# Attention probabilities of 6 of 16 pairs of heads turned by VectorE in 32x32 blocks and carried by DMA, in place of TensorE transposes

## The chip, the cores and the metric

One core of one Trainium2 chip runs the whole program, in one launch. The metric is the device time of an execution in microseconds (us). The kernel before took 1525.12 us in the median of three runs.

## The reference

Two sequences of 512 tokens with 1024 columns (`x_prompt` and `x_sample`) go through the same single layer with the same weights, all in float32:

```python
u = rmsnorm(h, norm_mix_g)
h = h + neighbourhood_attention(u, w_qkv, rpb, w_o)
u = rmsnorm(h, norm_ffn_g)
h = h + expert_choice_ffn(u, router_w, w_gate, w_up, w_down)
return rmsnorm(h, final_norm_g)
```

The attention has 16 heads of 64 columns. The tokens stand on a grid of 8 rows by 64 columns, and each token attends to the 8 rows of the 16 grid columns around it, with a bias per head and offset: `p = softmax(q k^T * 64**-0.5 + bias)`, then `p v`, then a product with `w_o`. The feed-forward part has 16 experts, each of which takes the 64 tokens of each sequence that score highest for it, through `silu(x w_gate) * (x w_up)` and `w_down` (1024 by 2048 columns).

## The kernel before

The two sequences are two trunks, b = 0 and 1, and their attention comes one after the other (up to about 450 us); then the experts run for both trunks together. Every engine has its own hand-written order of work, and the engines meet at counting semaphores. A float32 product is made of three products of rounded parts ("high" and "rest"): ScalarE (ACT) makes the high part (`w_high`, line 854, 1.9 us for a pair of weights of 1 MB), VectorE (DVE) the rest (`w_rest`, line 1380, 2.3 us), and TensorE (PE) multiplies (`products`, line 2063; `project_v`, lines 2111 and 2118).

In a trunk the 16 heads go in four groups of four (`first_group`, `second_group`, `third_group`, `last_group`, one function of each name per engine), a group in two pairs of heads: pair 0 is heads 0 and 1, pair 1 heads 2 and 3. The tokens are ordered by grid column, so a tile of 128 queries needs only a window of 256 keys. One step of the "head" loop, hh, holds both heads of the pair for half of the query tiles: 4 tiles of 128 queries by 256 keys, a row of 1024 floats in each of the 128 partitions. For a pair the work is:

- `score` (PE, line 2162): 24 matmuls of queries by keys into PSUM (banks 6 and 7 for hh even, 2 and 3 for hh odd).
- `biased` (DVE, line 1454): adds the bias, takes the maximum, writes `scores` (arena rows 3 and 0).
- `exponentials` (ACT, line 879), with the sum of each row.
- `normalise_rows` (DVE, lines 1468 and 1471): reciprocal and four multiplications.
- `turn_probabilities` (PE, line 2168): 64x64 transposes of the probabilities into the same PSUM banks, keys now in the partitions. The first pair of all takes 32 of them, every other pair 28, since blocks that no query needs are left out.
- `copy_pt`: DVE copies one PSUM bank of each half to `pt` (line 1462), ACT the other (line 884), 512 columns each.
- `values` (PE, line 2222): 16 matmuls of a pair, which the trace shows as 32 records, values as weights and probabilities as the moving side, into bank 4. They wait for both copies, in the first and third group also for `v_off`, a copy of `v` moved by 64 partitions, that two DMAs of ACT's queue make (lines 903 and 904, `shift_v`).

Between these steps PE works at projections: `project_v` (values of two groups, in the first and third group; v0 to v3, in banks 0, 1, 0, 1), `project_t` (q0, k0, q1, k1 of the next group; banks 5, 0, 1, 5) and `project_out` (w0 to w7, the product with `w_o`; banks 5, 0, 1 in turn). A bank is opened for a job (`open_job`) when DVE or ACT has copied what was in it (`copy_q`, `copy_k`, `copy_v`, `add_out`). ACT's `group_values` (first and third group) has the order copy_v 0, copy_v 1, copy_pt 0, copy_pt 1, copy_v 2, copy_v 3, shift_v. A wait on ACT or DVE holds back all that stands behind it on that engine. Weights come by DMAs of SP's queue as slots of `raw` come free (`load`, line 496: a load waits until DVE has made the rest of what was there).

Order of PE in the second group, before: w0 to w5, turn pair 0, w6 and w7, values of pair 0, score of pair 1, q0, k0, turn pair 1, q1, values of pair 1, scores of the next group's pair 0, k1.

Of the kernel before, what the change touches and what calls it, by code (L numbers as in the profile page):

```python
# [24 lines left out]
P = 128  # L25
# [7 lines left out]
HEADS = 16  # L33
HD = D // HEADS
# [82 lines left out]


def jobs_before(b, g, bank):
# [45 lines left out]
TABLE_BANKS = ((4, 4), (6, 4))  # L165
ROW_BANKS = (4, 6)


def encoder_kernel(nc, x, x_t, g_mix, g_ffn_col, g_ffn, g_fin, w_qkv, bias, w_o, router_w, w_gate, w_up, w_down, identity, y):
# [5 lines left out]
    with ExitStack() as ctx:  # L175
# [80 lines left out]
        scores = [arena[:, r, :].rearrange("p (i k) -> p i k", i=TILES) for r in (3, 0)]  # L256
        pt = (arena[:, 2, :], arena[:, 1, :])
        rt = (v[:, :, :].rearrange("p i n -> p (i n)"), arena[:, 1, :])
        squares_junk = arena[:, 3, :]
# [66 lines left out]
        q_high, q_rest = sem("q_high"), sem("q_rest")  # L326
        k_high = sem("k_high")
        diag_done = sem("diag_done")
# [48 lines left out]
        pt_mm = sem("pt_mm")  # L377
        pt_act, pt_dve = sem("pt_act"), sem("pt_dve")
        pv_mm = sem("pv_mm")
        rinv_done = sem("rinv_done")  # L380
# [469 lines left out]
        def _(act):  # L850
# [31 lines left out]
            def copy_pt(A, hh):  # L882
                act.wait_ge(pt_mm, A + hh + 1)
                nc.scalar.copy(pt[hh % 2][:, 512:1024], bank(PAIR_BANKS[hh % 2] + 1)).then_inc(pt_act, 1)

            def cast_qk(b, g, what, m):
# [99 lines left out]
            def group_values(b, g):  # L986

                copy_v(b, g, 0)
                copy_v(b, g, 1)
                copy_pt(head_count(b, g), 0)  # L990
                copy_pt(head_count(b, g), 1)
                copy_v(b, g, 2)
                copy_v(b, g, 3)
                shift_v(b, g)
# [27 lines left out]
            def second_group(b):  # L1022
                A = head_count(b, 1)
                exponentials(A, 0)
                exponentials(A, 1)
                cast_qk(b, 1, "q", 1)
                cast_qk(b, 1, "k", 1)
                next_high(b, 1, None, "v", 2)
                copy_pt(A, 0)
                copy_pt(A, 1)  # L1030
                if b == 0:
                    next_piece(2)
                    next_piece(3)
                next_high(b, 1, "w7", "v", 3)
                split_ot(A, 1, 0)
                exponentials(A, 2)
                exponentials(A, 3)
                if b == 0:
                    next_piece(4)
                copy_pt(A, 2)  # L1040
                copy_pt(A, 3)
                cast_qk(b, 2, "q", 0)
                cast_qk(b, 2, "k", 0)
                if b == 0:
                    next_piece(5)
                split_ot(A, 1, 1)
                next_high(b, 1, "q1", "w", 1)
# [53 lines left out]
            for kc in range(KC):  # L1101
                if kc % 2 == 0:
# [6 lines left out]
                                     scale=g_col[:, kc:kc + 1]).then_inc(uth_done, 1)  # L1109
            first_high(1, 0, K_PARTS, wk_in, k_high)  # L1110
            first_high(1, 1, K_PARTS, raw_in[1], high_done)
# [264 lines left out]
        def _(dve):  # L1376
# [83 lines left out]
            def copy_pt(A, hh):  # L1460
                dve.wait_ge(pt_mm, A + hh + 1)
# [92 lines left out]
            def first_group(b):  # L1554
# [44 lines left out]
            def second_group(b):  # L1599
# [32 lines left out]
            def third_group(b):  # L1632
# [5 lines left out]
                copy_last_k(b, g)  # L1638
                normalise_rows(A, 1)
                rest_pair(b, "q", 3)  # L1640
                copy_pt(A, 0)
                copy_pt(A, 1)
                rest_qk(b, g, "q", 1)
# [140 lines left out]
            for kc in range(KC):  # L1784
# [6 lines left out]
                split_x(0, kc, kc + 1)  # L1791
            first_rest(1, 0, K_PARTS, k_high, 1, q_rest)
            first_rest(1, 1, K_PARTS, high_done, 2, rest_done)
# [263 lines left out]
        def _(pe):  # L2057
# [86 lines left out]
            def score(A, b, g, hh):  # L2144
# [4 lines left out]
                if not (isinstance(A, int) and A + hh < PAIRED):  # L2149

                    pe.wait_ge(pt_dve, A + hh - 1)
                    pe.wait_ge(pt_act, A + hh - 1)
                for i in range(HALF_TILES):
# [39 lines left out]
            def values(A, b, g, hh):  # L2193

                p, half = hh // 2, hh % 2
                pe.wait_ge(pt_dve, A + hh + 1)
                pe.wait_ge(pt_act, A + hh + 1)
                if half == 0 and not (isinstance(A, int) and A + hh == 0):
# [12 lines left out]
                for i in range(HALF_TILES):  # L2211
                    tile = HALF_TILES * half + i
                    row = WIN_COL[tile] * ROWS
                    probabilities = pt[half].rearrange("p (r n t) -> p r n t", r=2, n=2 * TILES)
                    first = FIRST_CHUNK[tile]
                    for c in (first, 1 - first):
                        lo, hi = NEEDS[tile][c][0], NEEDS[tile][c][-1] + 1
                        for a in range(PAIRED):
                            n, head = 2 * (HALF_TILES * a + i) + c, PAIRED * p + a
                            vals = (v_off_all if row % P else v_all)[:, g % SHARED, row // P + c, head * HD:(head + 1) * HD]  # L2220
                            out = bank(4)[a * HD:(a + 1) * HD, tile * P + lo * HD:tile * P + hi * HD].rearrange("p (r t) -> p r t", r=hi - lo)
                            last = nc.tensor.matmul(out, vals, probabilities[:, lo:hi, n, :], start=c == first, stop=c != first)  # L2222
                last.then_inc(pv_mm, 1)

            def first_group(b):
# [22 lines left out]
            def second_group(b):  # L2248
# [12 lines left out]
                project_t(b, g, "k0", k)  # L2261
                turn_probabilities(A, 2)
                project_t(b, g, "q1", q)
                values(A, b, g, 2)
                values(A, b, g, 3)
                score(B, b, g + 1, 0)
                score(B, b, g + 1, 1)
                project_t(b, g, "k1", k)

            def third_group(b):  # L2270
# [3 lines left out]
                project_v(b, g, 0, v)  # L2274
                turn_probabilities(A, 0)
                project_v(b, g, 2, v)
# [441 lines left out]
```

## Time and profile before

| what | us |
|---|---|
| median of 3 runs (lowest, highest) | 1525.12 (1524.8, 1525.46) |
| the profiled execution, its own time | 1524.84 |
| its span in the profile | 1523.0 |
| TensorE busy | 1510.3 (99%) |
| VectorE busy | 1311.9 (86%) |
| ScalarE busy | 1215.8 (80%) |

The profile is of one execution; times in it count from the start of its span. The granted TensorE clock was 0.999 of full speed. PE is a matmul, PEld its weight load, SPq and ACTq are the DMAs that SP and ACT issue. An operation's duration on PE is longer than its share of the time, since matmuls overlap; the distance between two starts is what one costs.

### The profile page before, as it was taken

What the parts mean: (1) busy time and instruction counts of PE and PEld (TensorE: products, weight loads), DVE (VectorE), ACT (ScalarE), POOL (GpSimd) and SP (SyncE); (2) the same over time, 40 slices, a digit from 0 to 9 for tenths busy, and PEclk for the clock granted to TensorE, in tenths of its full rate; (3) what the DMA queues carried; (4) which work ended last, traced back from release to release, by engine and by line L of the source; (5) the groups of instructions that cost most, each with busy time, mean ns of one, the idle gap of its engine ahead of it and who ended that gap; (6) DMA issues with size and microseconds to landing.
All of it is one profiled execution on the core that took longest, in us unless ns stands there. A gap on an engine that the chain in (4) does not pass through costs nothing.

```text
span 1523.0 us, 22253 instructions
## 1 busy us (share of the span) xinstructions
PE 1510.3 (99%) x7854; PEld 1221.3 (80%) x7854; DVE 1311.9 (86%) x1415; ACT 1215.8 (80%) x1435; POOL 329.7 (22%) x154
## 2 busy tenths in 40 slices
PE   9999999999999999999999999999999999999997
PEld 7888878888873788888888888888888888888886
DVE  7684786685766899999999999999999999999988
ACT  6453656344454689999999999999999999999997
POOL 0000001000012232242322423233242322420103
PEclk9999999999999999999999999999999999999999
DMA  9533537333476999999999999999999999999998
GB/s 346 187 136 123 159 139 277 110 125 98 138 241 229 396 420 397 411 395 412 399 406 405 398 409 395 402 402 404 403 392 407 403 398 407 395 412 381 393 388 354
DMA packets 156407, 498.60 MB, mean 327 GB/s; under 512 B 10880, under 2 KB 36608, under 8 KB 156352
## 3 DMA queue, kind: packets, MB, share of 16 engines
q1 hardware_dynamic: 144624, 461.54, 77.4%
q0 software_dynamic: 9280, 31.07, 6.7%
q10 hardware_dynamic: 2448, 5.25, 1.3%
q8 instruction: 35, 0.57, 0.1%
q14 instruction: 20, 0.16, 0.0%
HBM read 473.70 MB, written 20.97 MB: 325 GB/s over the span
## 4 chain that ended last, share of the span: by engine, by line
PE 90%; ACT 3%; DVE 2%; DMA 2%; issue 2%; SPq 0%; POOLq 0%; POOL 0%; DVEq 0%; ACTq 0%
PE ps L2063 77%; PE ps L2111 4%; PE ps L2118 2%; PE ps L2222 2%; PE ps L2162 1%; ACT w_high L1229 1%; PE ps L2380 1%; DVE w_rest L1380 1%; PE ps L2168 1%; DMA raw<-w_up 1%; ACT arena L1200 1%; DMA u_rows<-arena 1%; DMA raw<-w_qkv 0%; PE ps L2662 0%; PE ps L2376 0%
## 5 line engine op out<-in xcount | busy, mean ns | idle before, releaser
L1380 DVE TENSOR_TENSOR w_rest<-raw,w_high 128x2048 fp32r<-128x2048 f32 x212 | 477.9, 2283 | 42.3 <-ACT w_high L1229 25.1
L1229 ACT CAST w_high<-raw 128x2048 fp32r<-128x2048 f32 x184 | 352.1, 1915 | 17.5 <-PE ps L2063 14.6
L2063 PE MATMUL ps<-w_high,xt_high 128*128 128x512 f32 x984 | 305.2, 390 | 0.7 <-DVE w_rest L1380 0.6
L2063 PE MATMUL ps<-w_rest,xt_high 128*128 128x512 f32 x984 | 304.4, 389 | 0.0
L2063 PE MATMUL ps<-w_high,xt_rest 128*128 128x512 f32 x984 | 304.2, 389 | 0.0
L2063 PEld LDWEIGHTS ps<-w_high,xt_high 128*128 128x128 f32 x984 | 184.1, 188 | 41.5 <-DVE w_rest L1380 2.4
L1380 DVE TENSOR_TENSOR w_rest<-early,w_high 128x2048 fp32r<-128x2048 f32 x90 | 204.4, 2285 | 13.3 <-ACT w_high L1229 13.3
L2063 PEld LDWEIGHTS ps<-w_rest,xt_high 128*128 128x128 f32 x984 | 184.7, 188 | 38.5
L2063 PEld LDWEIGHTS ps<-w_high,xt_rest 128*128 128x128 f32 x984 | 184.7, 188 | 38.5
L1380 DVE TENSOR_TENSOR w_rest<-raw_more,w_high 128x2048 fp32r<-128x2048 f32 x92 | 205.9, 2273 | 4.7 <-ACT w_high L1229 4.7
L1200 ACT COPY arena<-arena 32x256 f32<-32x256 f32 x464 | 187.3, 404 | 10.7
L1229 ACT CAST w_high<-early 128x2048 fp32r<-128x2048 f32 x90 | 172.2, 1915 | 10.8 <-PE ps L2063 8.9
L1229 ACT CAST w_high<-raw_more 128x2048 fp32r<-128x2048 f32 x92 | 175.8, 1912 | 3.0 <-PE ps L2063 1.9
L811 POOL DMA_INDIRECT h_rows<-xh,rows x15 | 109.6, 7305 | 303.4 <-ACT xh L1211 303.4
L768 POOL DMA_INDIRECT xh<-u_rows,aff x60 | 136.5, 2275 | 82.4 <-DVE v L1880 54.6
L2063 PE MATMUL ps<-ut_high,w_high 128*128 128x512 f32 x240 | 96.2, 401 | 0.3 <-DVE w_rest L1523 0.3
L2063 PE MATMUL ps<-ut_rest,w_high 128*128 128x512 f32 x240 | 93.7, 390 | 0.0
L2063 PE MATMUL ps<-ut_high,w_rest 128*128 128x512 f32 x240 | 93.5, 390 | 0.0
L879 ACT ACTIVATE arena<-arena,nmx 128x256 f32<-128x256 f32 x128 | 63.3, 496 | 32.3 <-DVE nmx L1458 32.2
L2063 PE MATMUL ps<-w_high,ht_high 128*128 128x512 f32 x256 | 78.9, 389 | 0.0
L2063 PE MATMUL ps<-w_rest,ht_high 128*128 128x512 f32 x256 | 78.8, 389 | 0.0
L2063 PE MATMUL ps<-w_high,ht_rest 128*128 128x512 f32 x256 | 78.8, 389 | 0.0
(317 smaller groups left out, 2273.1 us busy)
## 6 DMA issues: line engine op xcount, KB each, us to landing
raw<-w_down SPq DMA_DIRECT2D x64, 1024.0 KB, 8.6
raw<-w_gate SPq DMA_DIRECT2D x62, 1024.0 KB, 8.5
raw<-w_up SPq DMA_DIRECT2D x62, 1024.0 KB, 9.2
raw_more<-w_down SPq DMA_DIRECT2D x32, 1024.0 KB, 7.6
early<-w_down SPq DMA_DIRECT2D x32, 1024.0 KB, 8.0
raw_more<-w_gate SPq DMA_DIRECT2D x31, 1024.0 KB, 9.7
raw_more<-w_up SPq DMA_DIRECT2D x31, 1024.0 KB, 7.7
early<-w_gate SPq DMA_DIRECT2D x31, 1024.0 KB, 9.4
```

Of the source, the lines that this page charges most:

```text
L768: pool.indirect_dma_start(xg[:, t * SPAN:(t + 1) * SPAN], None, u_pieces, at).then_inc(gathered, 16)
L811: pool.indirect_dma_start(h_dram, bass.IndirectOffsetOnAxis(ap=rows[:, e:e + 1], axis=0), ys, None, compute_op=ALU.add).then_inc(scattered ...
L879: nc.scalar.activation(scores[hh % 2][:, i, :], scores[hh % 2][:, i, :], ACT.Exp, bias=nmx[:, hh % 2, i:i + 1], accum_out=psum_row[:, hh % ...
L1200: nc.scalar.copy(to_chunks[columns, :, tokens], from_blocks[tokens, :, columns]).then_inc(turn_step[h], 1)
L1229: nc.scalar.copy(w_high[:, i % SLOTS, :], src).then_inc(high_done, 1)
L1380: nc.vector.tensor_tensor(w_rest[:, j, :], src, w_high[:, j, :].bitcast(F32), ALU.subtract).then_inc(rest_done, 1)
L2063: done = nc.tensor.matmul(out, lhs, rhs, start=start and part == 0, stop=stop and part == 2)
L2111: nc.tensor.matmul(out[i], tokens[:, at], w_high[:, j:j + SHARED, kc * GC:(kc + 1) * GC], start=kc == 0 and tokens is ut_high, stop=False)
L2118: last = nc.tensor.matmul(out[i], ut_high[:, at], w_rest[:, j:j + SHARED, kc * GC:(kc + 1) * GC], start=False, stop=kc == KC - 1)
L2162: last = nc.tensor.matmul(bank(PAIR_BANKS[half], 2)[:, at + begin:at + end], queries[on, tile * P:(tile + 1) * P], keys[on, lo + begin:lo ...
L2168: return nc.tensor.transpose(bank(PAIR_BANKS[half] + r)[:, at:at + HD], scores[half][on, i, c * P:(c + 1) * P], ident[on, on])
L2222: last = nc.tensor.matmul(out, vals, probabilities[:, lo:hi, n, :], start=c == first, stop=c != first)
```

## The change

For pairs (group 0, pair 0), (group 1, pair 1) and (group 2, pair 0) of each trunk, 6 of 16, the transposes of TensorE and the four copies out of PSUM go. In their place DVE turns each half's 128x1024 floats in blocks of 32x32 (`turn_blocks_pt`), and 16 DMAs of ACT's queue per pair (`move_pt`), each of 32 partitions by two pieces of 1 KB (64 KB), bring the blocks to their partitions, in the arena rows of `scores`. ACT waits for DVE's second turn before it issues them. `values` waits for all 16 and reads probabilities in four parts of 32 columns, not two of 64. In the second group PE's k1 product moves from behind the next group's scores to ahead of the values, and DVE turns ahead of `rest_pair(b, "v", 2)`. `project_v` waits for its second bank only when it comes to it. One semaphore (`k_high`) is merged into another.

```diff
+BY_BLOCKS = ((0, 0), (1, 1), (2, 0))
+        moved_pt = (arena[:, 3, :], arena[:, 0, :])
...
@@ ScalarE @@
+            def move_pt(A):
+
+                act.wait_ge(pt_dve, A + PAIRED)
+                for n in range(MOVES):
+                    a, c = n % QUARTERS, n // QUARTERS
+                    queries, keys = slice(a * QUARTER, (a + 1) * QUARTER), slice(c * QUARTER, (c + 1) * QUARTER)
+                    into, of = arena[keys, 0:TILES:TILES - 1, a * WIN:(a + 1) * WIN], arena[queries, 1:TILES - 1, c * WIN:(c + 1) * WIN]
+                    act.dma_start(into, of).then_inc(pt_moved, 16)
...
                 copy_v(b, g, 0)
                 copy_v(b, g, 1)
-                copy_pt(head_count(b, g), 0)
-                copy_pt(head_count(b, g), 1)
+                move_pt(head_count(b, g))
                 copy_v(b, g, 2)
                 copy_v(b, g, 3)
                 shift_v(b, g)
...
                     next_piece(4)
-                copy_pt(A, 2)
-                copy_pt(A, 3)
+                move_pt(A + PAIRED)
                 cast_qk(b, 2, "q", 0)
                 cast_qk(b, 2, "k", 0)
...
@@ VectorE @@
+            def turn_blocks_pt(A, hh):
+
+                dve.wait_ge(norm_done, TILES * (A + hh + 1))
+                probabilities = scores[hh % 2].rearrange("p i (c b j) -> p b (i c) j", c=2, b=QUARTERS)
+                nc.vector.transpose(pt[hh % 2], probabilities).then_inc(pt_dve, 1)
...
                 normalise_rows(A, 1)
+                turn_blocks_pt(A, 0)
+                turn_blocks_pt(A, 1)
                 if b == 0:
                     rest_qk(b, g, "q", 1)
...
-                copy_pt(A, 0)
-                copy_pt(A, 1)
                 rest_qk(b, g, "k", 1)
...
+                normalise_rows(A, 2)
+                turn_blocks_pt(A, 2)
+                normalise_rows(A, 3)
+                turn_blocks_pt(A, 3)
                 rest_pair(b, "v", 2)
-                normalise_rows(A, 2)
-                normalise_rows(A, 3)
                 copy_q(b, g, 0)
                 rest_pair(b, "v", 3)
                 copy_k(b, g, 0)
-                copy_pt(A, 2)
-                copy_pt(A, 3)
...
@@ TensorE @@
-                out = [bank(open_job(b, g, f"v{i}")).rearrange("p (a n) -> p a n", a=SHARED) for i in (lo, lo + 1)]
+                out = [bank(turn(b, g, f"v{i}")[0]).rearrange("p (a n) -> p a n", a=SHARED) for i in (lo, lo + 1)]
...
                 for i in (0, 1):
+                    open_job(b, g, f"v{lo + i}")
                     for kc in range(KC):
...
-                pe.wait_ge(pt_dve, A + hh + 1)
-                pe.wait_ge(pt_act, A + hh + 1)
+                if by_blocks(A + hh):
+                    pe.wait_ge(pt_moved, 16 * MOVES * (turned_by_blocks(A + hh - half) // PAIRED + 1))
+                else:
+                    pe.wait_ge(pt_dve, A + hh + 1)
+                    pe.wait_ge(pt_act, turned_whole(A + hh) + 1)
...
                 project_v(b, g, 0, v)
-                turn_probabilities(A, 0)
                 project_v(b, g, 2, v)
...
                 project_t(b, g, "k0", k)
-                turn_probabilities(A, 2)
                 project_t(b, g, "q1", q)
+                project_t(b, g, "k1", k)
                 values(A, b, g, 2)
                 values(A, b, g, 3)
                 score(B, b, g + 1, 0)
                 score(B, b, g + 1, 1)
-                project_t(b, g, "k1", k)
```

The third group loses its first `turn_probabilities` in the same way, and its DVE order changes like the first group's.

## Rows read from the trace of the kernel before

**Rows 1.** The page: the chain that ended last, by engine

```profile
PE 90%; ACT 3%; DVE 2%; DMA 2%; issue 2%; SPq 0%; POOLq 0%; POOL 0%; DVEq 0%; ACTq 0%
```

**Rows 2.** Busy time in one stretch, trunk 0's groups: length; PE, PEld, DVE, ACT, POOL; clock, DMA

```profile
30.00:205.00 175.00, 174.93 (x1232) 143.67 (x1233) 123.51 (x337) 92.47 (x206) 1.97 (x3) 1.00 0.49 164
```

**Rows 3.** Waits of SP's queue in the experts' part (from 560 us)

```profile
SPq L510 <- DVE w_rest L1380: 725.8, 339, 4.4
```

**Rows 4.** Chain that ended last in order of time: start, us, what

```profile
42.61 1.14 PE ps L2168 x32
...
65.75 1.69 PE ps L2222 x32
...
100.50 11.13 PE ps L2063 x48
111.63 1.01 PE ps L2168 x28
```

**Rows 5.** Timeline of PE around one turn in the second group

```profile
111.01 0.39 PE L2063 MATMUL ps<-ut_rest,w_high 128*128 128x512 f32 x1
111.24 0.39 PE L2063 MATMUL ps<-ut_high,w_rest 128*128 128x512 f32 x1
...
112.57 0.50 PE L2063 MATMUL ps<-ut_high,w_high 128*128 128x512 f32 x1
112.91 0.40 PE L2063 MATMUL ps<-ut_rest,w_high 128*128 128x512 f32 x1
```

**Rows 6.** Groups by line: DVE's copy, and its transpose of this size in the experts

```profile
L1462 DVE COPY arena<-ps 128x512 f32<-128x512 f32 x32 | 20.8, 685 | 17.9 <-PE ps L2168 17.8
...
L1880 DVE STREAM_TRANSPOSE v<-xh 128x1024 f32<-128x1024 f32 x13 | 16.0, 1233 | 0.0
```

**Rows 7.** Timeline of ACT's queue: DMAs issued one behind the other

```profile
55.69 0.70 ACTq L903 DMA_DIRECT2D v_off<-v  x1
56.42 0.62 ACTq L904 DMA_DIRECT2D v_off<-v  x1
57.24 1.07 ACTq L933 DMA_DIRECT2D piece<-x  x1
```

**Rows 8.** Timeline of SP's queue, 15 DMAs in a row: first, second and third, last

```profile
0.76 0.43 SPq L591 DMA_DIRECT2D raw<-w_qkv  x1
1.24 0.93 SPq L596 DMA_DIRECT2D early<-x_t  x2
...
8.20 0.86 SPq L599 DMA_DIRECT2D ident<-identity  x1
```

**Rows 9.** Issue to landing: the two DMAs of v_off (lines 903, 904; 384 KB each), one of 4 KB

```profile
DMA to landing us min/median/max: 3.9/4.0/4.0
...
DMA to landing us min/median/max: 5.0/5.0/5.1
...
g_col<-g_mix ACTq DMA_DIRECT2D x1, 4.0 KB, 2.6
```

**Rows 10.** Timeline, second group of trunk 0: ACT's last exponentials of each head, DVE's normalising

```profile
106.43 0.19 ACT L879 ACTIVATION_READ_ACCUMULATOR arena<-arena,nmx 128x1 f32 x1
...
108.40 0.18 ACT L879 ACTIVATION_READ_ACCUMULATOR arena<-arena,nmx 128x1 f32 x1
...
108.27 0.17 DVE L1468 RECIPROCAL rinv<-psum_row 128x4 f32<-128x4 f32 x1
...
109.53 0.17 DVE L1468 RECIPROCAL rinv<-psum_row 128x4 f32<-128x4 f32 x1
```

**Rows 11.** Timeline, second group of trunk 1: ACT's fourth exponential, PE's turn

```profile
326.41 0.19 ACT L879 ACTIVATION_READ_ACCUMULATOR arena<-arena,nmx 128x1 f32 x1
...
334.03 1.08 PE L2168 MATMUL ps<-ident,arena 64*128 64x64 f32 x28
```

**Rows 12.** Timeline of ACT, third group of trunk 0: values copied

```profile
138.12 0.69 ACT L896 ACTIVATE v<-ps,rstd 128x512 f32<-128x512 f32 x1 [1.12 <-PE ps L2118]
...
148.43 0.69 ACT L896 ACTIVATE v<-ps,rstd 128x512 f32<-128x512 f32 x1 [8.58 <-PE ps L2118]
```

More of the change, by code:

```diff
@@ L116, in b_last, with by_blocks, turned_whole, turned_by_blocks @@
     return b + 1 < TRUNKS or kind != "last"
+def by_blocks(n):
+    return (n % HEADS // GROUP, n % GROUP // PAIRED) in BY_BLOCKS
+def turned_whole(n):
+    return sum(not by_blocks(m) for m in range(n))
+def turned_by_blocks(n):
+    return sum(by_blocks(m) for m in range(n))
 def jobs_before(b, g, bank):
@@ L326, in encoder_kernel @@
         q_high, q_rest = sem("q_high"), sem("q_rest")
-        k_high = sem("k_high")
         diag_done = sem("diag_done")
@@ L378, in encoder_kernel @@
         pt_act, pt_dve = sem("pt_act"), sem("pt_dve")
+        pt_moved = sem("pt_moved")
         pv_mm = sem("pv_mm")
@@ L882, in copy_pt @@
             def copy_pt(A, hh):
-                act.wait_ge(pt_mm, A + hh + 1)
+                act.wait_ge(pt_mm, turned_whole(A + hh) + 1)
                 nc.scalar.copy(pt[hh % 2][:, 512:1024], bank(PAIR_BANKS[hh % 2] + 1)).then_inc(pt_act, 1)
+            def move_pt(A):
[5 more added lines that the diff above has]
+                    act.dma_start(into, of).then_inc(pt_moved, 16)
             def cast_qk(b, g, what, m):
@@ L1109, in _ @@
                                      scale=g_col[:, kc:kc + 1]).then_inc(uth_done, 1)
-            first_high(1, 0, K_PARTS, wk_in, k_high)
+            first_high(1, 0, K_PARTS, wk_in, q_high)
             first_high(1, 1, K_PARTS, raw_in[1], high_done)
@@ L1460, in copy_pt @@
             def copy_pt(A, hh):
-                dve.wait_ge(pt_mm, A + hh + 1)
+                dve.wait_ge(pt_mm, turned_whole(A + hh) + 1)
                 nc.vector.tensor_copy(pt[hh % 2][:, 0:512], bank(PAIR_BANKS[hh % 2])).then_inc(pt_dve, 1)
+            def turn_blocks_pt(A, hh):
+                dve.wait_ge(norm_done, TILES * (A + hh + 1))
+                probabilities = scores[hh % 2].rearrange("p i (c b j) -> p b (i c) j", c=2, b=QUARTERS)
+                nc.vector.transpose(pt[hh % 2], probabilities).then_inc(pt_dve, 1)
             def normalise_rows(A, hh):
@@ L1639, in third_group @@
                 normalise_rows(A, 1)
+                turn_blocks_pt(A, 0)
+                turn_blocks_pt(A, 1)
                 rest_pair(b, "q", 3)
-                copy_pt(A, 0)
-                copy_pt(A, 1)
                 rest_qk(b, g, "q", 1)
@@ L1791, in _ @@
                 split_x(0, kc, kc + 1)
-            first_rest(1, 0, K_PARTS, k_high, 1, q_rest)
+            first_rest(1, 0, K_PARTS, q_high, Q_PARTS, q_rest)
             first_rest(1, 1, K_PARTS, high_done, 2, rest_done)
@@ L2151, in score @@
                     pe.wait_ge(pt_dve, A + hh - 1)
-                    pe.wait_ge(pt_act, A + hh - 1)
+                    pe.wait_ge(pt_act, turned_whole(A + hh - 1))
                 for i in range(HALF_TILES):
@@ L2213, in values @@
                     row = WIN_COL[tile] * ROWS
-                    probabilities = pt[half].rearrange("p (r n t) -> p r n t", r=2, n=2 * TILES)
+                    parts = QUARTERS if by_blocks(A + hh) else 2
+                    wide, each = P // parts, parts // 2
+                    probabilities = (moved_pt if by_blocks(A + hh) else pt)[half].rearrange("p (r n t) -> p r n t", r=parts, n=2 * TILES)
                     first = FIRST_CHUNK[tile]
@@ L2220, in values @@
                             vals = (v_off_all if row % P else v_all)[:, g % SHARED, row // P + c, head * HD:(head + 1) * HD]
-                            out = bank(4)[a * HD:(a + 1) * HD, tile * P + lo * HD:tile * P + hi * HD].rearrange("p (r t) -> p r t", r=hi - lo)
-                            last = nc.tensor.matmul(out, vals, probabilities[:, lo:hi, n, :], start=c == first, stop=c != first)
+                            out = bank(4)[a * HD:(a + 1) * HD, tile * P + lo * HD:tile * P + hi * HD].rearrange("p (r t) -> p r t", t=wide)
+                            last = nc.tensor.matmul(out, vals, probabilities[:, each * lo:each * hi, n, :], start=c == first, stop=c != first)
                 last.then_inc(pv_mm, 1)
@@ L2274, in third_group @@
                 project_v(b, g, 0, v)
-                turn_probabilities(A, 0)
                 project_v(b, g, 2, v)
```

## The prediction

> **What bounds the kernel now.** I read the page first, then stretches, then order in time. The chain that ended last is TensorE for 90% of the span [rows 1], and in trunk 0's groups TensorE is busy 174.93 of 175.00 us, VectorE 123.51 and ScalarE 92.47, and the DMA engines run at 0.49 of their share [rows 2]. So in the stretch that the change touches TensorE is the bound, and what comes off its queue comes off the time, as long as nothing that it waits for gets late. The experts behind it do not take the gain back: there SP's queue waits 725.8 us for buffers that VectorE has not yet freed [rows 3], so loads follow the computing and shift with it. The chain in order of time [rows 4] shows the turns as pieces of their own, on the path.
>
> **The transposes that go.** The first pair's 32 take 1.14 us, every other pair's 28 take 1.01 us [rows 4]. That is not all: the last product ahead of the turn starts at 111.24, the first behind it at 112.57 and the next at 112.91. Undisturbed products start 0.23 us apart (111.01 to 111.24), so without the turn the second one would start at 111.69 and not at 112.91: a turn costs 1.22 us, of which 0.21 is getting into it and out of it [rows 5]. Six turns, one of them the long one: 1.35 + 5 x 1.21 = 7.4 us, all on the path.
>
> **The product that moves.** k1 (24 products, 24 x 0.227 = 5.4 us) moves from behind the next scores to ahead of the values. It loses the switch that stood ahead of it and `project_v` gets that switch in its place: nothing. The merged semaphore is counted in the same order: nothing.
>
> **Values read in four parts.** 16 matmuls a pair, 32 records, take 1.69 us, 53 ns a record [rows 4]. The columns are the same in number. No row has four parts; the turns' records of 64 columns cost 1.01 / 28 = 36 ns each, so if a record of four parts cost as much as two such short ones it would be 72 and not 53 ns: 6 x 32 x 19 ns = 3.7 us at most, and nothing at least. I take nothing: the nearest row is this line itself, which reads two parts apart already.
>
> **VectorE.** Twelve copies of 0.685 go (8.2 us), twelve transposes of 128x1024 floats come, 1.233 each by the row in the experts whose input is as strided [rows 6]: 14.8 us, so 6.6 more in all, 3.3 a trunk, beside 51 us that it stands idle in 175 [rows 2]. The transposes stand ahead of work that has slack: in the first group the rest of q1's and k1's casts and two weight rests, which nobody wants before `project_v` is through.
>
> **ScalarE and its queue.** Twelve copies go; 96 DMAs come. Each issue keeps ScalarE's instruction stream for a time i. The sixteen of a pair stand one behind the other, ahead of copy_v 2 and 3 and `shift_v`, or of the casts of q0 and k0. The bounds for i: ScalarE's own two SBUF-to-SBUF DMAs start 0.73 us apart, and a third behind them takes 1.07 [rows 7]; SP's run of 15 begins with 0.43 and two in 0.93, and from the first start to the last is 7.44 us for 14 intervals, 0.53 each [rows 8]. I take 0.53, since that is the one long run of small transfers, 256 KB or less for most, and keep 0.47 (two in 0.93) and 0.73 as ends, with 1.07 for a rival. The 48 issues of a trunk are then 25 us, beside 82 us of idle ScalarE in the same stretch. From issue to landing the last one takes between 2.6 us (4 KB alone) and 5.0 (the second of v_off) [rows 9]; I take 4.0, the first of v_off, which has no other of its queue ahead of it but carries 384 KB and not 64.
>
> **What is late next, second group, trunk 0** (times of the trace of before; the gain of the first group shifts all of them alike). Head 2's last exponential is through at 106.62. A `normalise_rows` costs 1.26 us (108.27 to 109.53), `rest_pair` v2 no longer stands ahead of it, and head 3's exponentials end at 108.58, in time [rows 10]. So normalise, turn, normalise, turn: 106.7 + 1.3 + 1.23 + 1.3 + 1.23 = 111.8. ScalarE's issues go from 111.85 to 111.85 + 16 i, and all has landed at 111.85 + 15 i + 4.0: with 0.53, at 123.8. TensorE has q0 and k0 behind it at 111.63 [rows 4]; q1 and k1 bring it to 111.63 + 2 x 5.44 = 122.5, where it wants the values. It waits **1.3 us**. In trunk 1 the same exponential ends at 326.60, and the turns so at 331.75, but q0 and k0 end at 334.1 [rows 11] and k1 at 345.0; the moves have landed at 331.85 + 8.0 + 4.0 = 343.8. No wait. The difference of 2.5 us between the trunks is the squares and pieces of x that ScalarE does in trunk 0 only.
>
> **First and third group.** Let E be the end of `project_v`'s first half. In the third group copy_v 1 starts at E and takes 0.69, the moves end at E + 0.7 + 16 i, and copy_v 2, whose bank is full at E + 9.1 (148.43 less the turn of 1.22 is 147.2, E is 138.12, [rows 12]), is through at E + 1.4 + 16 i = E + 9.9. TensorE wants bank 0 for w1 after the second half (48 x 0.227 = 10.9) and w0 (1.4), at E + 12.2. No wait until i is 0.675. In the first group bank 0 is wanted later, for k0, but v_off has to land before the values at E + 21.8: its second DMA is issued near E + 2.8 + 16 i and takes 5.0, so E + 7.8 + 16 i = E + 16.3 (about one us later in trunk 0, where VectorE's second turn and not copy_v 1 sets the start). No wait. The moves themselves have landed long before. `project_v`'s second half starts 1.2 us earlier; copy_v 0 has freed bank 0 by then, and copy_v 1, which ends 0.7 us too late for it, frees the bank that is now waited for 16 products (3.6 us) later. That edit costs and gives nothing, but without it 0.7 us of each such turn would stay as a wait.
>
> **Sum.** -7.4 + 1.3 = -6.1 us. The profiled execution's own time is 1524.84, 1.84 above its span; it gives 1518.7. The median of before is 0.28 higher, so against it the forecast is **1519.0 us**. About 0.2%, 3.05 us, is what a measurement of this kernel can tell from no change.
>
> The trace shows 2.6 us and 4.0 us from issue to landing [rows 9]. The Trainium skill, "DMA: Bandwidth & Descriptors", section "Anatomy of one DMA", puts a fixed 2.0 us on a DMA of the GpSimd path plus its bytes at 436 GB/s; for 64 KB an estimate by it is 2.15 us, the wait of 1.3 would be gone and the sum -7.4. The rows show nothing under 2.6 [rows 9].
>
> **Rivals.**
> - *Full cover.* i at 0.47, or a landing near 2.6: the wait in trunk 0 is 111.85 + 7.05 + 4.0 - 122.5 = 0.4 or, at 0.53, 111.85 + 7.95 + 2.6 - 122.5 = 0. Time 1517.7. For it: the DMA engines are half idle. Against: v_off's 4.0. Chance 0.25.
> - *The gain is eaten in the second group.* i at v_off's pace, 0.67 to 0.73: at 0.70 trunk 0 waits 3.9, trunk 1 15 x 0.70 - 9.15 = 1.3, and the third groups wait 16 x 0.70 - 10.8 = 0.4 each: 6.0 of 7.4, time 1523.7. For it: the same queue, SBUF to SBUF, two pieces a partition, as the moves have. Or the four-part reading costs its 3.7. Against: these are the only two of their kind. Chance 0.15.
> - *Slower: ScalarE's issues set the pace.* The waits grow with i at four places: (15 i - 6.65) + (15 i - 9.15) + 2 x (16 i - 10.8). They reach 7.4 at i = 0.72 and 10.5, slower by 0.2%, at i = 0.77; from 0.81 on v_off is late in the first groups too. At i = 1.0: 8.35 + 5.85 + 10.4 + 3.0 + 2.0 = 29.6, time 1547. For it: the 1.07 of the third DMA in a row on this queue [rows 7], and SP's loads of 1 MB share the DMA engines. Against: that one stood behind 768 KB on its way, a pair's moves are 64 KB each, and DMAs are busy only half of the stretch. Chance 0.15. A rule of the Trainium skill, "VectorE: DVE Perf Modes", section "Rules for kernel authors", is on this rival's side: it gives a 128x128 transpose to TensorE if PSUM will do as destination, and only 32x32 blocks to VectorE. The trace agrees as to work (1.01 us a pair against 2.5 us of VectorE and 16 DMAs) and so far not as to the path, since only TensorE is full.
> - *It does not do what it says*: the turns stay on the path in another form, such as TensorE standing where the turn stood. Only if banks are late, which the reading above excludes. Chance 0.02, within 0.2%.
>
> **How the numbers follow.** The forecast has 0.43. Its own range is -4 to -7 us (i up to 0.6, landing up to 5.0). Faster by over 0.2%: 0.43 + 0.25, and nothing of the rest, 0.68. Within 0.2%: 0.15 + 0.02, 0.17. Slower: 0.15. The range goes from 1517.0 (full cover and the 0.28 of the run) to 1525.0, so that it holds the forecast, full cover and the eaten gain, and leaves out the slower case and the worst of the eaten one.
>
> **What would show it.** Right: the group of `turn_half` has 452 - 172 = 280 records. The chain shows no turn between `project_v`'s halves in the first and third group, and one piece of 96 products ahead of the second group's last values; a wait of TensorE for a DMA of arena, once, near 122 us, of about 1.3. ACTq shows 96 DMAs arena to arena, about 0.5 us apart. VectorE's transposes of 1.2 us stand at arena from arena. Wrong: starts of those DMAs 0.7 us or more apart, TensorE waiting at `project_out` for ScalarE's copy of v, values records longer than 53 ns apart, a turn taking over 1.5 us on VectorE, or any lengthening behind 450 us.

## The result, and the profile after

The kernel with the change takes **1533.09 us** (median of 5 runs, 1532.5 to 1535.18), the kernel before 1525.12 (5 runs, 1524.69 to 1525.46): a ratio of 1.0056, 95% interval 1.0045 to 1.0068. It is slower by 8.0 us. The forecast was 1519.0, with a range up to 1525.0 and a chance of 0.15 for slower. It was wrong in sign, and the result lies out of its range.

The profiled execution of the change took 1535.18 us, with a span of 1533.3 against 1523.0, so its rows show 2.1 us more than the median. First its page: busy time of each engine, and the chain that ended last by engine (this answers [rows 1]).

```profile
PE 1509.7 (98%) x7682; PEld 1221.5 (80%) x7682; DVE 1318.7 (86%) x1415; ACT 1208.8 (79%) x1423; POOL 329.6 (21%) x154
...
PE 81%; ACT 5%; DVE 4%; ACTq 4%; DMA 3%; issue 2%; SPq 0%; POOLq 0%; POOL 0%; DVEq 0%
```

TensorE has 172 matmul records fewer (7854 to 7682), but the chain is now TensorE for 81% and not 90%; ACTq and DMA have come in with 4% and 3%. Next TensorE's waits in the attention (from 30 to 450 us), with the sum in us, how often, and the longest:

```profile
PE ps L2258 <- DMA arena<-arena: 8.7, 2, 5.4
PE ps L2093 <- DVE xh L1524: 0.9, 2, 0.6
PE ps L2258 <- DMA v_off<-v: 0.8, 1, 0.8
```

Before, TensorE's waits in this stretch came to 0.5 us, none of them for a DMA. Now TensorE stands 8.7 us in two places, once per trunk, ahead of the second pair's values of the second group. The chain in order of time (start, us, what) leads there; this is trunk 0, to be held against [rows 4]:

```profile
110.19 1.26 DVE arena L1492
111.47 0.65 ACTq L910
...
121.34 6.36 DMA arena<-arena
...
127.75 3.25 PE ps L2258 x20
131.00 2.55 PE ps L2193 x14
```

Three things are to be seen. VectorE's last turn ends at 111.45, close to what was worked out (111.8). The sixteen issues take 0.66 us each, and the last lands 6.36 us after it was issued. And the values and scores behind the wait take 3.25 and 2.55 us, where the same work took 1.69 and 1.53 before. In trunk 1 the last move lands after 6.54 us, and the two take 3.25 and 2.56. The windows around the wait say why the work is slow (columns as in [rows 2]; the third figure from the end is the granted clock, then the share of the DMA engines and GB/s):

```profile
110.00:115.00 5.00, 5.00 (x24) 4.14 (x23) 4.96 (x5) 0.00 (x0) 0.00 (x0) 1.00 0.37 93
115.00:120.00 5.00, 5.00 (x24) 4.14 (x23) 2.01 (x2) 0.00 (x0) 0.00 (x0) 1.00 1.01 347
120.00:125.00 5.00, 2.39 (x11) 1.65 (x9) 1.90 (x3) 1.76 (x4) 0.00 (x0) 1.00 1.06 335
...
128.00:130.00 2.00, 2.00 (x24) 2.00 (x24) 0.00 (x0) 0.00 (x0) 0.00 (x0) 0.50 0.04 8
130.00:132.00 2.00, 2.00 (x22) 1.88 (x20) 0.33 (x1) 0.94 (x2) 0.00 (x0) 0.50 0.00 0
```

The same windows of the kernel before:

```profile
110.00:115.00 5.00, 5.00 (x47) 3.97 (x46) 5.00 (x9) 2.22 (x4) 0.00 (x0) 1.00 1.04 382
115.00:120.00 5.00, 5.00 (x49) 4.11 (x47) 2.36 (x4) 0.72 (x2) 0.00 (x0) 1.00 0.78 293
120.00:125.00 5.00, 5.00 (x39) 4.28 (x40) 4.27 (x22) 4.42 (x11) 0.00 (x0) 1.00 0.00 1
```

With the change the DMA engines are full from 115 to 125, just when most of the moves go (before, they were full from 110 to 115 and empty from 120 to 125), and after the wait TensorE runs at half its clock (0.50, that is 1.2 GHz of 2.4). What fills the DMA engines stands in SP's queue. First the change, then the kernel before:

```profile
113.64 0.37 SPq L513 DMA_DIRECT2D raw<-w_qkv  x1
...
116.44 0.38 SPq L513 DMA_DIRECT2D raw<-w_o  x1
```

```profile
108.38 0.37 SPq L496 DMA_DIRECT2D raw<-w_qkv  x1
...
113.70 0.38 SPq L496 DMA_DIRECT2D raw<-w_o  x1
```

The first is the 1 MB load of the next group's k weights (k3). It waits for VectorE's `rest_pair(b, "v", 2)`, which the change puts behind the two turns. It starts 5.3 us later, and its bytes and those of the next load (w_o) are on their way together with the moves. In trunk 1 it starts at 338.63; before, 328.35, which is 5.6 us later once the 4.6 us are taken off that the whole of trunk 1 has slipped (its first values start at 292.77, before at 288.13).

ScalarE in the third group, against [rows 12] (timeline):

```profile
144.71 11.17 ACTq L910 DMA_DIRECT2D arena<-arena  x16
155.97 1.26 ACT L922 ACTIVATE v<-ps,rstd 128x512 f32<-128x512 f32 x2 [10.58 <-issue]
```

The sixteen issues take 11.17 us. One of them takes 1.42 us; the others start 0.65 us apart, as in the second group. In trunk 1's third group the sixteen take 10.40 us (0.65 each), but the second issue of v_off behind them takes 1.78, where the others take 0.63 (chain):

```profile
382.52 1.78 ACTq L930
```

Both delays reach TensorE by the same way, here in trunk 0 (chain):

```profile
158.74 1.92 ACT w_high L871
...
160.68 1.23 DVE w_rest L1410
161.91 0.61 DVE xh L1524
...
162.56 4.38 PE ps L2093 x18
```

ScalarE makes the high part of the next weights (`w_high`) late, VectorE waits for it before the rest (`w_rest`), the addition into xh stands behind that, and TensorE waits for the bank that this addition empties, with 18 of the 48 products of `project_out` still to do. From the end of `project_v`'s first half to the values it is 22.26 us in trunk 0 and 22.65 in trunk 1. Before it was 22.99, or 21.77 less the turn, so the third groups lose 0.5 and 0.9 us.

The moves (line 910) and VectorE's turns (line 1492) by line; the first answers to [rows 7, 9], the second to [rows 6]:

```profile
L910 ACTq DMA_DIRECT2D arena<-arena x96: 592/619/1586, 44.4 to 379.8; - x96
```

```profile
L1492 DVE STREAM_TRANSPOSE arena<-arena 128x1024 f32<-128x1024 f32 x12 | 14.4, 1229 | 0.1
```

**Where the time went.** Nothing that counts happens in the experts. Their first store (u_rows, the gate to the gathers) starts at 459.54 before and 468.59 after, 9.05 of the 10.3 us of span; SP's wait for VectorE there is 731.6 us against 725.8 [rows 3]. For the attention: −7.4 for the turns; +8.7 for the waits for moves; +5.2 for values and scores at half clock (3.25 + 2.55 against 1.69 + 1.53, twice); +1.1 for v_off in trunk 0's first group; +1.4 in the third groups. That is 9.0 of 9.05.

### The profile page after: what moved, and what is told of

Its sections match the earlier page's. It is cut to its first block, busy times and chain, and to the rows that moved or that the text cites. A ratio compares the mean times of both kernels' runs of the same rounds, so it can differ in the third digit from the quotient of the medians.

```text
span 1533.3 us, 21981 instructions
## 1 busy us (share of the span) xinstructions
PE 1509.7 (98%) x7682; PEld 1221.5 (80%) x7682; DVE 1318.7 (86%) x1415; ACT 1208.8 (79%) x1423; POOL 329.6 (21%) x154
## 4 chain that ended last, share of the span: by engine, by line
PE 81%; ACT 5%; DVE 4%; ACTq 4%; DMA 3%; issue 2%; SPq 0%; POOLq 0%; POOL 0%; DVEq 0%
PE ps L2093 71%; ACTq L910 3%; ACT w_high L1253 2%; PE ps L2142 2%; PE ps L2258 2%; PE ps L2193 1%; PE ps L2413 1%; PE ps L2149 1%; DVE w_rest L1404 1%; DMA arena<-arena 1%; ACT arena L1224 1%; DMA u_rows<-arena 1%; DVE arena L1478 1%; PE ps L2199 1%; ACT w_high L871 0%
## 5 line engine op out<-in xcount | busy, mean ns | idle before, releaser
L1253 ACT CAST w_high<-early 128x2048 fp32r<-128x2048 f32 x90 | 172.2, 1915 | 10.9 <-PE ps L2093 8.9
```

The source lines that it names most:

```text
L1253: nc.scalar.copy(w_high[:, i % SLOTS, :], src).then_inc(high_done, 1)
```

## The experiments

Each edit is to the kernel with the change, unless said otherwise. "Store" is the start of the store of u_rows in the profile, 459.54 before and 468.59 with the change: it holds the attention alone. It is a figure of one execution, the profiled one, and the time of the table is a median.

| kernel | median us (runs) | of before in the same batch | ratio, 95% | store at |
|---|---|---|---|---|
| first and third group alone | 1520.95 (7) | 1525.06 | 0.9973 [0.9962, 0.9984] | 455.75 |
| second group alone | 1536.45 (4) | 1525.06 | 1.0073 [1.0058, 1.0088] | 472.52 |
| loads held back | 1522.35 (10) | 1525.06 | 0.9980 [0.9971, 0.9990] | 455.11 |
| products in the wait | 1531.09 (4) | 1525.06 | 1.0039 [1.0024, 1.0055] | 465.57 |
| moves shared, second group | 1519.61 (7) | 1524.72 | 0.9968 [0.9957, 0.9979] | 454.48 |
| moves shared, all groups | 1519.56 (6) | 1524.72 | 0.9968 [0.9955, 0.9980] | 453.06 |
| k1 not moved | 1544.58 (4) | 1524.72 | 1.0127 [1.0112, 1.0143] | 478.76 |
| `rest_pair` v2 in its old place | 1525.25 (10) | 1524.72 | 1.0000 [0.9990, 1.0010] | 458.64 |
| moves shared, second and third | 1518.80 (5) | 1524.95 | 0.9958 [0.9945, 0.9972] | 452.62 |
| the same, both banks up front | 1522.92 (11) | 1524.95 | 0.9987 [0.9978, 0.9996] | 456.55 |

From the store to the end of the span it is 1063.2 to 1065.3 us in the twelve profiles, 1063.5 in the kernel before. A difference of a us or so between a row's store and its time lies in that spread, which was not followed.

**1 and 2: the change by halves.** The change is made for the first and third group alone, or for the second alone; the other groups keep their order of before.

```diff
-BY_BLOCKS = ((0, 0), (1, 1), (2, 0))
+BY_BLOCKS = ((0, 0), (2, 0))
```

> Only the first pairs of the first and third group go by blocks (4 of 16 pairs); the second group is as before the change. Theory A (the loss sits in the second group: the moves land late, TensorE stands and its clock falls afterwards): four turns save 1.35 + 3 x 1.21 = 5.0 us, of which v_off's delay in trunk 0 (1.1) and late copies of v in the third groups (0.5 to 0.7 each) give back 2.3; about 1522.4, faster by 2 to 3.5 us. Theory B (the block route costs wherever it stands, by the values in four parts, VectorE's turns or traffic): no faster than before, 1525 or more.

```diff
-BY_BLOCKS = ((0, 0), (1, 1), (2, 0))
+BY_BLOCKS = ((1, 1),)
```

> Only the second pair of the second group goes by blocks (2 of 16 pairs), k1 moved as in the change. Theory A: two turns save 2.4 us, TensorE stands 5.4 + 3.3 us for the moves and loses 2 x 2.6 us at the lower clock behind that: 11 us slower than before in sum, 1534 to 1537. Theory B: a third of the loss of the whole change, about 3 us, 1528.

Measured: 1520.95 and 1536.45. The first is faster than before, by more than theory A asked. The halves are worth −4.1 and +11.4 us against before, 7.3 together, and the whole change 8.0: they add up, so the loss is the second group's alone. Theory A had counted 0.5 to 0.7 us for late copies of v in each third group of the first kernel. There was none of it (21.76 us from the end of the first half to the values in both trunks): its sixteen issues take 10.41 and 10.49 us, with no long one among them or behind them. Of the second kernel the wait of TensorE from 30 to 450 us, and its chain of waits in trunk 0:

```profile
PE ps L2282 <- DMA arena<-arena: 11.0, 2, 7.6
```

```profile
122.78 7.42 DMA arena<-arena
...
130.24 3.26 PE ps L2282 x32
133.50 1.52 PE ps L2217 x24
```

Here the first group has saved nothing, the last move is issued 1.4 us later than in the whole change, and it lands after 7.42 us. The values run at half clock again, but the scores behind them take 1.52 us, as at full clock: after this longer wait (7.6 us) the low clock cost 1.6 us and not 2.6. In its trunk 1, after 3.4 us of waiting, the two take 3.26 and 2.63. The four turns of the other half gain 4.1 of the 5.0 that they are worth (1.35 + 3 x 1.21).

**3: the loads behind the moves.** SP waits until the second group's moves have landed before it loads k3 and all that follows in its queue.

```diff
                 load_bias(b, 2, 0)
+                sp.wait_ge(pt_moved, 16 * MOVES * (3 * b + 2))
                 load_nth(n + 5)
```

> The whole change, but SP's queue waits for the second group's moves to have landed before it loads k of the last group and what follows (k3, bias, w2), so that no load of 1 MB is released beside the moves. Theory A1 (the last move lands 6.4 us after its issue because the loads share the DMA engines): landing 2.6 to 4 us, the wait falls to 2 to 3 us in trunk 0 and under 1 us in trunk 1, the clock stays up or nearly so: 1520 to 1525. Rival A2 (the queue's own sixteen DMAs make the backlog): landing stays above 5.5 us and the time at 1533.

Measured: 1522.35, faster than before, 10.7 us off the change by one wait in another queue. Its chain in trunk 0, and the DMA share in two windows:

```profile
120.58 2.06 DMA arena<-arena
...
122.68 1.76 PE ps L2259 x32
```

```profile
115.00:120.00 5.00, 5.00 (x24) 4.14 (x23) 1.36 (x2) 0.00 (x0) 0.00 (x0) 1.00 0.38 97
120.00:125.00 5.00, 3.93 (x50) 3.25 (x50) 1.90 (x3) 2.27 (x6) 0.00 (x0) 1.00 0.43 107
```

With the DMA engines at 0.38 the last move lands in 2.06 us, not 6.36, the wait is 1.1 us, once, and behind it TensorE keeps its clock: 1.76 us for the values. So the long landing time is contention with the loads, and not a property of the moves or of their own queue.

**4: products in the wait.** TensorE does 24 more products of 128x512 ahead of the values, into a bank that the values overwrite; nothing reads them. They fill the wait.

```diff
                 project_t(b, g, "k1", k)
+                pe.wait_ge(ot_done, 2 * (GROUPS * b + g) + 1)
+                for _ in range(FILLING):
+                    nc.tensor.matmul(bank(4), ut_high[:, 0:P], ut_high[:, 0:T], start=True, stop=True)
                 values(A, b, g, 2)
```

> The whole change, with 24 products of 128x512 that nobody reads (5.4 us of TensorE) ahead of the second group's last values, in PSUM bank 4 before the values overwrite it. If the slow values and scores behind the wait (3.25 and 2.55 us in place of 1.69 and 1.53) come from TensorE's clock after it stood: granted clock 1.00 there, values 1.7 us, 5.2 us less, against about 2 us of filling too much in trunk 1: 1529 to 1531. If they come from reading the probabilities in four parts: values stay at 3.2 us, and the time is 1533 or more, up to 1536.

Measured: 1531.09, 2.0 us faster than the change although TensorE has 48 products more to do. Its chain in trunk 0, and the clock of a window there:

```profile
121.06 7.52 DMA arena<-arena
...
128.62 1.76 PE ps L2259 x32
130.39 1.54 PE ps L2194 x24
```

```profile
128.00:130.00 2.00, 1.38 (x28) 1.38 (x29) 0.00 (x0) 0.00 (x0) 0.00 (x0) 1.00 0.02 6
```

The move lands later than in the change (7.52 us), but the granted clock is 1.00, and values and scores take 3.3 us and not 5.8. So the 2.6 us a trunk were the clock, and the clock had fallen because TensorE stood.

**5: half of the moves on SP's queue, second group.** ScalarE issues 8 of the 16, SP the other 8, in front of its load of k3.

```diff
+            def move_share(g, A):
+                if g not in SHARING:
+                    return
+                sp.wait_ge(pt_dve, A + PAIRED)
+                for n in range(8, MOVES):
+                    ...
+                    sp.dma_start(into, of).then_inc(pt_moved, 16)
...
                 load_bias(b, 2, 0)
+                move_share(1, head_count(b, 1) + PAIRED)
                 load_nth(n + 5)
```

> The whole change, but in the second group ScalarE issues eight of the sixteen moves and SP the other eight, ahead of its load of k3. Theory (issues of 0.66 us in one line, and loads released beside them): the last issue comes 5 us earlier, near 116.8 of the trace's time, the last move lands 2 to 3 us later, ahead of TensorE, which no longer stands in the second group; all of 8.7 us of waits and 5.2 us of low clock go: 1518.5 to 1520. If the moves were slow by themselves (both queues share what limits them): landing stays over 5 us, TensorE waits 1 to 3 us, 1523 or more.

Measured: 1519.61, where it was expected. (Its runs fall in two groups, four at 1519.1 to 1519.6 and three at 1521.4 to 1521.7; the profiled one is of the second.) The two queues side by side (timelines of ScalarE's queue and of SP's), and the landing times of SP's share:

```profile
111.40 5.25 ACTq L928 DMA_DIRECT2D arena<-arena  x8
```

```profile
111.39 5.55 SPq L638 DMA_DIRECT2D arena<-arena  x8
116.98 0.60 SPq L514 DMA_DIRECT2D raw<-w_qkv  x1
```

```profile
DMA to landing us min/median/max: 2.0/2.0/2.3
```

An issue costs as much on SP (0.69) as on ScalarE (0.66), so it is not the engine that makes it dear; whether it is the form of the move alone was not tried, and k3's load behind the moves costs 0.60 here and 0.37 in the change. But two queues issue at the same time, the pair's issues are over in 5.5 us, and k3's load is behind them by itself. TensorE doesn't wait there in either trunk.

**6: the same in all three groups.** The diff is `SHARING = (0, 1, 2)`, with the calls at the places of the other two groups in SP's order.

> As e5, in the first and third group too: eight moves each by ScalarE and SP. If the issues on ScalarE's stream are what delays v_off and the copies of v (1.1 us in trunk 0's first group, 0.5 us in each third group), another 1 to 2 us goes against e5: 1517 to 1518.5. If SP's loads, now later, become the wait (SP stands for VectorE's turns ahead of loads), it is slower than e5.

Measured: 1519.56, a us short of what was expected and not to be told from 1519.61. The third groups' loss was gone (21.76 us from the end of the first half to the values in both trunks), and the store is 1.4 us earlier than in number 5, of which the time shows nothing. In trunk 0's first group TensorE waited anew, before the values:

```profile
PE ps L2276 <- DVE early L1524: 0.8, 1, 0.8
```

**7: k1 not moved.** The products of k1 go back behind the next group's scores.

```diff
-                project_t(b, g, "k1", k)
                 values(A, b, g, 2)
                 values(A, b, g, 3)
                 score(B, b, g + 1, 0)
                 score(B, b, g + 1, 1)
+                project_t(b, g, "k1", k)
```

> The whole change, but k1's product back behind the next group's scores. TensorE wants the values 5.4 us earlier in each trunk and stands 5.4 us longer for the same landing: 8.7 + 10.9 us of waits, the clock loss behind them as before: 1542 to 1545. If the time did not grow by 8 us or more, the wait for the landing would not be what sets the time there.

Measured: 1544.58, 11.5 us over the change, and TensorE's wait for the moves is longer by the 5.4 us of k1 in each trunk:

```profile
PE ps L2258 <- DMA arena<-arena: 19.6, 2, 10.8
```

So k1's products do cover the moves one for one. They explain 10.9 of the 11.5 us, and nothing shows a cost of moving them.

**8: `rest_pair` v2 in its old place**, ahead of the normalising and the turns of the second group, so that k3's load starts early but the moves late.

```diff
+                rest_pair(b, "v", 2)
                 normalise_rows(A, 2)
                 turn_blocks_pt(A, 2)
                 normalise_rows(A, 3)
                 turn_blocks_pt(A, 3)
-                rest_pair(b, "v", 2)
```

> The whole change, but VectorE makes the rest of v2 ahead of the second group's normalising, as before the change: the load of k3 is released 5 us earlier, the turns come 1.9 to 2.3 us later. If each load of 1 MB beside the moves delays their landing by some 2 us, the two cancel: 1531 to 1535. If the later turns alone count, 4 us more: 1537. If the contention weighs more than the turns, under 1530.

Measured: 1525.25, the same as before the change and 7.8 us faster than with it. (One of its ten runs took 2466.74 us, which nothing here explains; the other nine took 1523.1 to 1526.4, and the median doesn't rest on it.) In trunk 0, the loads in SP's queue, and the chain:

```profile
107.54 0.37 SPq L513 DMA_DIRECT2D raw<-w_qkv  x1
...
115.38 0.38 SPq L513 DMA_DIRECT2D raw<-w_o  x1
```

```profile
122.40 2.02 DMA arena<-arena
...
124.47 2.31 PE ps L2258 x32
126.77 2.56 PE ps L2193 x15
```

The last move is issued 1.06 us later than in the change (122.40 against 121.34) and lands 4.3 us sooner (2.02 against 6.36). The expectation that weighed the later turns more than the contention was wrong. The wait is now 2.5 us here and 0.3 in trunk 1, and even behind 2.5 us the scores run at half clock (2.56 us).

**9: shared in the second and third group, ScalarE alone in the first.** The diff is `SHARING = (1, 2)`.

> The moves are shared with SP in the second and third groups and left to ScalarE in the first. Theory (ScalarE's run of sixteen issues of 0.65 us is what the third groups lose by, 0.5 to 0.7 us each, and in the first group sharing gives nothing): the third groups' values start without a wait as in the kernel with all groups shared, the wait of 0.7 us for early in trunk 0's first group is gone, time 1518 to 1519.5. Rival (the third groups are no limit, the remaining differences are spread over the experts): 1519.5 to 1520.5, as with the second group alone shared.

Measured: **1518.80**, the lowest median of all, though its interval overlaps those of numbers 5 and 6; the store is 6.9 us earlier than before the change. TensorE's waits from 30 to 450 us have come down to these:

```profile
PE ps L2469 <- ACT gv L1009: 0.5, 1, 0.5
PE ps L2111 <- DVE xh L1542: 0.3, 1, 0.3
PE ps L2276 <- DMA v_off<-v: 0.2, 1, 0.2
PE ps L2211 <- DVE qk L1590: 0.2, 1, 0.2
```

**10: the same kernel, but `project_v` waits for both banks up front**, as before the change.

```diff
-                out = [bank(turn(b, g, f"v{i}")[0]).rearrange("p (a n) -> p a n", a=SHARED) for i in (lo, lo + 1)]
+                out = [bank(open_job(b, g, f"v{i}")).rearrange("p (a n) -> p a n", a=SHARED) for i in (lo, lo + 1)]
...
-                    open_job(b, g, f"v{lo + i}")
```

> As the kernel before it (moves shared in the second and third groups), but project_v waits for both of its banks ahead of its first product, as before the change. Theory of the prediction: copy_v 1 ends about 0.7 us behind the point where the second half wants to start, in the first and third groups of both trunks, so the time is 4 x 0.7 = 2.8 us more than with the waits apart, 1521 to 1522.5, and TensorE shows four waits for ScalarE's copy of v of 0.5 to 0.8 each. Rival (the copy is done in time, or what is lost is given back at the next wait): within 0.5 us of the kernel before it, and no such waits.

Measured: 1522.92, 4.1 us over number 9 and a little over the expected range; the store is 3.93 us later, 0.98 for each of the four. The waits are where they were expected:

```profile
PE ps L2159 <- ACT v L940: 3.5, 4, 0.9
```

So the smallest edit of the change is worth 4.1 of the 6.2 us that number 9 gains. That it is worth nothing as long as the turn stands there is the prediction's argument; no run has it in the kernel before.

## Why the prediction was wrong, step by step

- **What bounds: right.** TensorE was the bound, and most of what was taken off it came off the end: in number 9 the store is 6.9 us earlier, of 7.4 forecast for six turns (1.22 by [rows 5]), and the time 6.2.
- **VectorE: right.** Twelve turns of 1.229 us (1.233 forecast, [rows 6]), through at 111.45 in the second group where 111.8 was forecast.
- **Values in four parts: right.** 1.69 us for 32 records at full clock (292.77 in trunk 1's first group), as in [rows 4]; the bound of 3.7 us was not needed. **The product that moves: right** (number 7). **`project_v` with split waits: right in kind**, 0.9 to 1.0 us a turn and not 0.7 (number 10).
- **The issue interval, i = 0.53: mis-sized.** It was taken from SP's run of small loads [rows 8], while v_off's pair on ScalarE's own queue (0.73 apart, [rows 7]) was the nearer row: the same engine, SBUF to SBUF, two pieces a partition. Measured: 0.66 in the second group, and 0.65 to 0.71 over the sixteen of the first and third groups. It made the second group's moves 15 x 0.13 = 1.9 us later. The closest rival, the gain eaten in the second group at i = 0.70, was nearest in this term, and its sum, 1523.7, was still 9.4 us too low.
- **The third groups: no wait forecast, 0.5 and 0.9 us measured.** The prediction's formula, 16 i − 10.8, stands for a wait for bank 0 ahead of w1, after ScalarE's copy of v. With 10.40 us of issues in trunk 1 it gives no wait, and the larger one was there. The way was another: one long issue (1.42 us, or 1.78 for v_off) delays `w_high`, that delays `w_rest` and the addition into xh, and TensorE waits for that. In number 1, without such an issue, nothing was lost.
- **The landing, 4.0 us: this is the step that failed most.** It was 6.4 and 6.5, and with the loads held back (number 3) 10.7 us of time came back, the wait and the low clock behind it together. The number was taken as a property of a DMA, from v_off, and it is one of what else is on its way: 2.06 with the loads held back, and up to 7.5 beside them (number 4). Why the loads were there is a step that the prediction did not take: moving `rest_pair` v2 behind the turns was counted as a gain for the turns and given no cost, but SP waits for it with the next loads, so the two transfers of 1 MB moved to where the moves are. The slower rival did name the loads of 1 MB that share the DMA engines, gave them no number, and was answered with a share of only half [rows 2]. That share is an average over 175 us; the windows show 0.37 from 110 to 115 us and 1.01 from 115 to 120. The trace of before had it to be read: windows at 1.04 and 0.78 and then at 0.00, and k3's load at 108.38 and w_o's at 113.70 in SP's queue.
- **The wait in trunk 0: 1.3 forecast, 5.4 measured.** 1.9 from the interval, 2.4 from the landing, less 0.35 by which VectorE was earlier, plus 0.2 by which TensorE was. **In trunk 1: none forecast, 3.3 measured**: with the 4.6 us that trunk 1 had slipped the moves should have landed at 343.8 + 4.6 = 348.4; they landed at 352.98, and TensorE wanted them at 349.7. Of these 4.6 us late, 2.0 are the interval and 2.5 the landing.
- **The price of standing: not thought of.** A wait was counted at its own length. It cost 2.6 us on top in each trunk, since TensorE's clock was at half level for the values and scores behind it (number 4). This term of 5.2 us, put at nothing, is nearly as large as the wait in trunk 0.
- **v_off in trunk 0's first group: no wait forecast, 0.8 measured**, 1.1 with the late start of the values: its second DMA was issued at 57.77, as 16 issues of 0.70 make it, and took 7.63 us and not 5.0. The share of the DMA engines was 1.11 from 58 to 62 us, against 0.82 before; that this is the reason was not tried.

The slower rival had a chance of 0.15, put on i of 0.77 or more. That was not the way it went: i was 0.65 to 0.71, and most of the loss is contention and clock. Two sums of the rivals are slightly off, and neither would move a chance: at i = 0.77 the waits come to 10.3 us and not 10.5, and full cover with its wait of 0.4 us gives 1518.1, while 1517.7 is the time without it. The rule of the Trainium skill named beside it ("VectorE: DVE Perf Modes", section "Rules for kernel authors": TensorE for a 128x128 transpose if PSUM will do as destination) came out right for this form of the change, at +8.0 us, and not for number 9, at −6.2 (1518.80 against 1524.95): where TensorE is the only full engine and the transfers are kept free, the other way pays. The other page, "DMA: Bandwidth & Descriptors" of the Trainium skill, section "Anatomy of one DMA", gave an estimate of 2.15 us for the landing of 64 KB, from its figures for the GpSimd path. The traces agree, on the queues of ScalarE and SP, where no load runs beside the moves (2.06 in number 3, and 2.0/2.0/2.3 for SP's share in number 5) and not where loads do (6.4 and 6.5). With a landing of 2.06 the kernel was 2.7 us faster than before.

Still open: the 1.3 us that the profiled execution loses behind the store lie in the spread that this stretch shows from profile to profile (1063.2 to 1065.3 us), and were not followed. Why single issues take 1.4 to 1.8 us, and why the low clock lasts longer behind some waits than behind others, no run shows.

## What to carry to other kernels

An operation that nobody on the bound engine waits for can still be the gate of a queue: before moving it, look which loads it releases, and what they will run beside. A DMA's time to landing is to be read from a stretch that is as loaded as the one where it will go, so read the DMA share in windows of 5 us and not over a stage. And where many small DMAs stand between an engine and its data, split their issue over two queues and put the loads behind them: the same idea went from 8.0 us slower to 6.2 us faster by that alone. A wait of the bound engine may cost more than its length: look at the granted clock and at the durations behind it.

## What was not expected of the hardware

- After a wait of 5.4 us the granted TensorE clock was 0.50 for some 6 us of work: 3.25 us for 32 records of values (1.69 at full clock) and 2.55 for 24 of scores (1.53). After 2.5 us of waiting (number 8) it fell too, and the scores took 2.56. After 1.1 us (number 3) there was nothing of it (1.76 and 1.53 us). A longer wait did not always cost more: after 7.6 us (number 2, trunk 0) the scores took 1.52 again, and after the second wait of number 7, of 8.8 us, 1.70.
- An SBUF-to-SBUF DMA of 32 partitions by two pieces costs its issuing engine 0.62 us on ScalarE (median, 592 to 1586 ns) and 0.60 on SP, where SP's 1 MB load of k3 costs 0.37 in the change (0.60 behind SP's moves, number 5). Now and then one issue costs 1.4 to 1.8 us.
- The same DMA of 64 KB lands in 2.06 us with the DMA engines at 0.4 of their share, and in 6.4 to 7.5 with two loads of 1 MB beside it, at 1.0.
